# Reordering the 32 attention units of a two-layer diffusion backbone: interleaved branches against one branch after the other

## The reference

```
def block_attention(q, k, v, scale):            # lax.map over blocks of 128 queries
        s = jnp.einsum('bqhgd,bkhd->bhgqk', qblk, k, preferred_element_type=jnp.float32) * scale
        p = jax.nn.softmax(s, axis=-1).astype(v.dtype)
        return jnp.einsum('bhgqk,bkhd->bqhgd', p, v)

def cd_attend(qc, qd, kc, vc, kd, vd, w_out):
    oc = block_attention(qc, kc, vc, HEAD_DIM ** -0.5)                # branch C, HEAD_DIM = 64
    od = block_attention(qd, kd, vd, (D_NOPE + D_ROPE) ** -0.5)       # branch D, 64 + 32 = 96
    return jnp.concatenate([oc, od], axis=-1) @ w_out
```

## Time and profile before

| what | value |
|---|---|
| median of three timed runs | 1846.65 us |
| profiled execution, its own time | 1846.65 us |
| its span | 1844.2 us |
| PE, PEld busy | 1697.8 us (92%), 1391.6 us (75%) |
| DVE, ACT busy | 1389.3 us (75%), 920.5 us (50%) |
| chain that ended last | PE 87%, DVE 6%, ACT 3% |
| mean granted TensorE clock | 0.954 |

### The profile page before, as it was taken

The page is one execution under the profiler, slowest core; times in us unless marked ns, Lnnn a source line. Parts: engine busy times, 40 slices in busy tenths (PEclk is TensorE's granted clock), DMA queues, the critical chain, the costliest instruction groups (busy, mean ns, idle before and its releaser), DMA issues.

```text
span 1844.2 us, 22480 instructions
## 1 busy us (share of the span) xinstructions
PE 1697.8 (92%) x8417; PEld 1391.6 (75%) x8418; DVE 1389.3 (75%) x1442; ACT 920.5 (50%) x844; POOL 0.2 (0%) x4
## 2 busy tenths in 40 slices
PE   4988899999999796897799999999899999999995
PEld 1876787888887595566688877888788887888884
DVE  5858757777787827673698977888698977888886
ACT  5421222221221424322577776777677676777773
POOL 0000000000000000000000000000000000000000
PEclk8988999999999798898799999999999999999998
DMA  9544333543675232001499998999899998999992
GB/s 353 188 151 138 119 102 130 181 146 128 212 236 191 64 115 69 24 1 40 142 355 338 354 339 296 344 343 357 281 347 342 358 333 289 350 344 357 334 358 99
DMA packets 214553, 426.38 MB, mean 231 GB/s; under 512 B 8187, under 2 KB 64029, under 8 KB 214453
## 3 DMA queue, kind: packets, MB, share of 16 engines
q1 hardware_dynamic: 210218, 420.37, 65.5%
q10 hardware_dynamic: 4234, 4.57, 0.8%
HBM read 423.86 MB, written 1.05 MB: 230 GB/s over the span
## 4 chain that ended last, share of the span: by engine, by line
PE 87%; DVE 6%; ACT 3%; issue 2%; DMA 1%; SPq 1%; DVEq 0%; ACTq 0%
PE bank L504 26%; PE bank L505 25%; PE bank L506 25%; PE bank L1740 2%; PE bank L1795 2%; PE bank L1729 2%; DVE lo L463 2%; PE bank L1834 1%; PE bank L1515 1%; DMA raw<-in_ada_w_dram 1%; PE bank L1746 1%; PE bank L1509 1%; ACT hi L457 1%; PE bank L1868 0%; PE bank L1869 0%
## 5 line engine op out<-in xcount | busy, mean ns | idle before, releaser
L463 DVE TENSOR_TENSOR lo<-raw,hi 128x2048 fp32r<-128x2048 f32 x361 | 820.8, 2282 | 223.8 <-ACT hi L457 222.2
L457 ACT ACTIVATE hi<-raw 128x2048 fp32r<-128x2048 f32 x361 | 689.3, 1912 | 490.1 <-PE bank L506 469.4
L505 PE MATMUL bank<-lo,xgh 128*128 128x512 f32 (+1 forms) x864 | 328.5, 380 | 13.4 <-issue 13.4
L504 PE MATMUL bank<-hi,xgh 128*128 128x512 f32 (+1 forms) x864 | 331.2, 383 | 9.5 <-DVE lo L463 6.3
L506 PE MATMUL bank<-hi,xgl 128*128 128x512 f32 (+1 forms) x864 | 327.7, 379 | 0.0
L505 PEld LDWEIGHTS bank<-lo,xgh 128*128 128x128 f32 x864 | 164.6, 191 | 46.2 <-issue 14.3
L504 PEld LDWEIGHTS bank<-hi,xgh 128*128 128x128 f32 x864 | 164.6, 190 | 43.0 <-DVE lo L463 6.5
L506 PEld LDWEIGHTS bank<-hi,xgl 128*128 128x128 f32 x864 | 164.5, 190 | 33.4
L504 PE MATMUL bank<-hi,aTh 128*128 128x512 f32 x396 | 159.1, 402 | 0.0
L506 PE MATMUL bank<-hi,aTl 128*128 128x512 f32 x396 | 154.8, 391 | 0.0
L505 PE MATMUL bank<-lo,aTh 128*128 128x512 f32 x396 | 154.3, 390 | 0.0
(11 more groups left out here) (316 smaller groups left out, 2197.8 us busy)
## 6 DMA issues: line engine op xcount, KB each, us to landing
raw<-in_moe_w_gate_dram SPq DMA_DIRECT2D x99, 1024.0 KB, 5.9
raw<-in_moe_w_up_dram SPq DMA_DIRECT2D x99, 1024.0 KB, 6.5
raw<-in_moe_w_down_dram SPq DMA_DIRECT2D x99, 1024.0 KB, 6.2
raw<-in_ada_w_dram SPq DMA_DIRECT2D x48, 1024.0 KB, 5.8
raw<-in_ffn_w_gate_dram SPq DMA_DIRECT2D x11, 1024.0 KB, 5.3
raw<-in_ffn_w_up_dram SPq DMA_DIRECT2D x11, 1024.0 KB, 5.4
raw<-in_ffn_w_down_dram SPq DMA_DIRECT2D x11, 1024.0 KB, 4.9
raw<-in_ab_w_in_dram SPq DMA_DIRECT2D x6, 1024.0 KB, 8.7
```

Source lines behind the costliest of these rows:

```text
L457: nc.scalar.activation(hi[n0 % SPL][:, 0:size], raw[slot][:, 0:size], ACT.Copy).then_inc(hi_ready, 1)
L463: nc.vector.tensor_tensor(lo[n0 % SPL][:, 0:size], raw[slot][:, 0:size], hi[n0 % SPL][:, 0:size].bitcast(F32), ALU.subtract).then_inc(lo_r ...
L504: nc.tensor.matmul(dst, lh, rh, start=first, stop=False, skip_group_check=True)
L505: nc.tensor.matmul(dst, lh, rl, start=False, stop=False, skip_group_check=True)
```

## The change

`unit(i)` is given another order, and `att_scale(i)` is written to fit. Before, the branch alternates with every unit; now all 16 units of branch C come first and then all 16 of branch D. Within a branch the order is as it was: head by head, and in each head the two blocks of queries.

```diff
         def unit(i):
 
-            return i % 2, i // 4, i // 2 % 2
+            return i // 16, i // 2 % 8, i % 2
 
         def att_scale(i):
-            return (96 if unit(i)[0] else 64) ** -0.5
+            return (64 if i < 16 else 96) ** -0.5
```

## The result

The changed kernel takes 1878.88 us (median of four runs, 1876.95 to 1879.54) against 1846.1 us (1845.39 to 1847.59, with a fourth run of the kernel before): a ratio of 1.0175, 95% interval 1.0157 to 1.0193. It is slower by 32.8 us, and the prediction was wrong. The profiled execution has a span of 1876.4 us.

The account below looks back on a forecast made before the run. TensorE was taken to bound the attention loop, with C's iterations 0.20 us longer than D's. From 1846.65 us, less 0.40 for units at full clock, plus 0.23 for unit 3, came 1846.5 us; range 1844.6 to 1848.6 us.

Parts of the forecast that it names:

- the steady term: Attention loop iterations: C costs 2.53 us and D 2.33 at full clock, whatever unit came before; change 0.
- The drain: Array emptying on either side of C's 64*128 scores in the attention loop, together 0.20 us for each unit of C.
- the first rival: Attention loop: the empty array is paid for the change of branch, so about 3.0 us go, 1843.6 us; chance 0.04.
- the second rival: Attention loop: DVE's copy becomes late in a run of D's units, +3.2 us, 1849.7 us; chance 0.04.
- the term on the half clock: Attention loop's slow start: unit 3 becomes C, losing 0.23 us if the clock rises as before, 0.46 if later.
- The third rival: Attention loop: the clock falls in the run of C's units, which use half the array's rows, +31 us, 1877 us; chance 0.03.

Follow-up runs that it names:

- e1: The kernel before with all 16 units of D first, then all 16 of C: 1849.73 us, ratio 0.9997 to the kernel before.
- e12: The changed kernel's order (C first), both branches' scores over all 128 rows, with zeros in the rest: 1844.12 us, ratio 0.9973.
- e7: The changed kernel with units 3 and 16 exchanged, so unit 3 is D and unit 16 is C: 1847.18, 1847.56, 1876.64 and 1877.67 us.
- e4: The kernel before with C and D alternating in runs of two units instead of one: 1870.55 us.
- e2: The changed kernel with C's scores over all 128 rows, C's keys held twice with zeros in the other half: 1847.07 us, ratio 0.9977.
- e9: e5 with rows 96 to 127 of D's queries and keys zero-filled, both products over 128 rows: 1824.94 us.
- e5: e1 with a small product of 96 rows by 16 columns ahead of each of D's scores: 1893.69 us.
- e6: The changed kernel with each of C's scores computed twice in a row, still with 64 rows: 1882.86 us.
- e15: The changed kernel run again without any edit: 1876.31 to 1879.56 us in four runs, ratio 1.0158.
- e10: D first as in e1, but both branches' scores over all 128 rows, with zeros in the rest: 1844.18 us, ratio 0.9976.
- e13: The kernel before plus 16 small products ahead of the last transposes of D's queries: 1825.28 us, ratio 0.9898.
- e11: The alternating order of the kernel before, both branches' scores over all 128 rows, with zeros in the rest: 1844.46 us, ratio 0.9976.

## Why the prediction was wrong

The views were read rightly, and the costs at full clock were met, in e1 though and not in the changed kernel. C's units at full clock cost 2.53 us, behind a C as behind a D, so the steady term of nothing holds. The drain is paid for the shape and not for the change of branch: e1 refutes the first rival, and in e12, where the shape is gone, a unit of C takes 2.33 us, the 0.20 less that I had read. (Its loop is 3.5 us shorter than before, 86.07 against 89.62; an earlier rise of the clock is in that too.) DVE was never late, in D's run in e1 either: the second rival falls.

The step that failed is one sentence in the term on the half clock: "If the clock rises at the same moment as before (755.00 us), what is lost is work at half speed". I took that moment as given, "for I see no reason for the clock to follow unit 3". It followed unit 3. This is the chain before the change, from where PE works without a wait; the scores at 752.85 are those of unit 3, of D, and the clock rises just after 755.0 us, during the values behind them:

```profile
750.03 1.97 PE bank L1740 x8
752.00 0.85 PE bank L1746 x4
752.85 1.71 PE bank L1729 x2
754.56 1.13 PE bank L1740 x8
```

The changed kernel works without a wait from 751.37 us on, with C's scores of 2.00 us at 754.19. There the rise did not come, and as every unit behind was of C, it didn't come until unit 16. With D put back as unit 3 alone (e7) it came in two runs of four, by their times. The term of 0.23 us was in truth 28.9. The price of a unit of C at half clock was too low as well, but that is small: 0.46 us over one of D in the prediction, 4.75 - 4.16 = 0.59 in the chains (4.16 = 1.71 + 1.60 + 0.85, e4).

The third rival had the time nearly right, 1877 us, and the way there wrong; part of that is luck, for it took twelve units at 5.1 us where thirteen took 4.75. It had the clock fall in C's run. e1 shows that it doesn't fall. Had I asked "does it rise?" instead, the stretch of 15.65 us at 0.50 ahead of it was in the first rows that I showed. I gave that rival 0.03 because PE "would be no less busy than before", and that was the wrong measure: 45.00 us busy of 45.00, at half clock. The argument that half of the array's rows might count was in the text; nothing in one trace could weigh it, so 0.03 was far too sure.

The range was also not quite what it says: half way to the first two rivals is 1844.5 and 1848.9 us, not 1844.6 and 1848.6. That changes nothing here.

On the cause itself: C's scores keep the clock down (e2), and with all rows in use for both branches the order costs nothing (e12). That the rows in use matter (e9 against e5) and that a small product's gap matters (e5 against e1) is shown each by itself, but on D's units. How much of C's case is its 64 rows and how much the emptying of the array around them, no run separates: e2 and e12 take away both, and e6 keeps both. The page TensorE: Matmul & The Clock Gate of the Trainium skill (section What's actually happening) has the clock set by how busy the PE has been recently. The profile's busy time is no such measure here: it reads 45.00 of 45.00 us at 0.50 after the change, and 30.00 of 30.00 from 770 to 800 us both in e5, at 0.50, and in e9, at 1.00.

What remains open: 2.4 us behind the loop in the changed kernel's profile, 2.0 in e15's. The clock in the first 91 us there is 0.76 in both, against 0.81 before. The 1.35 us ahead of the loop are not the change's: e15's loop starts 0.67 us earlier than the one before the change. Nothing was tried on the part behind, and it is within what the kernel before scatters by (1845.02 to 1862.78 us in 25 runs), part of which may be the same chance.

## What to carry to other kernels

Where TensorE runs at half clock, ask first what will raise it, and take nothing for granted there: an order that is neutral at full speed can keep the clock down for as long as it lasts. Fill unused rows with zeros where memory allows: here it made no product slower (0.86 us for the scores with 96 and with 128 rows), saved 0.20 us for each product of 64 rows, and none of the 30 runs of e10 to e12 missed the rise by anything that the time shows. And look at the turns of a long loop for stops that nothing explains; here 16 small products far ahead of the loop removed them.

## What the runs showed of the hardware that I had not expected

- A clock that is up was held by work that didn't raise it: 38 us of C's units at 1.00 in e1, 62 us of the same units at 0.50 after the change.
- Rows of zeros count as rows: they took D's run with small products from 0.50 to 1.00 (e5, e9). All six kernels whose first scores had 128 rows had the clock up for 3 to 7 us within the first iterations, and none of the eleven others.
- One program had two times 30 us apart (e7), in the profiled run with the clock's rise during a single unit.
- Three stops of 4.5 us on average and the clock's fall behind each, some 20 us, went away with 16 small products far ahead of the loop (e13); one wait more ahead of it moved them by one product (e11).
